# Two down projections by seven block products instead of eight

## The reference

```python
def swiglu(x, w_gu, w_down):
    g, u = jnp.split(x @ w_gu, 2, axis=-1)
    return (jax.nn.silu(g) * u) @ w_down

# second_block
f = swiglu(rms_norm_2(h, ffn1_pre_g[i]), ffn1_w_gu[i], ffn1_w_down[i])
h = h + 0.5 * rms_norm_2(f, ffn1_post_g[i])
z = rms_norm_2(h, attn_pre_g[i]) @ w_in[i] + b_in[i]
...
f = swiglu(rms_norm_2(h, ffn2_pre_g[i]), ffn2_w_gu[i], ffn2_w_down[i])
h = h + 0.5 * rms_norm_2(f, ffn2_post_g[i])
gate = jax.nn.sigmoid(rms_norm_2(h, ple_pre_g[i]) @ w_ple_gate[i])
```

## Time and profile before

| | us |
|---|---|
| median of 3 runs (lowest, highest) | 3358.51 (3353.12, 3361.56) |
| profiled execution, its own time | 3359.73 |
| its span, first to last instruction | 3357.9 |
| PE busy | 3182.2 (95%) |
| DVE, ACT, POOL busy | 1837.1, 1250.6, 1771.7 |

### The profile page before, as it was taken

How to read it: one execution, slowest core, us unless ns; L and a number is a source line. 1 busy time by engine, 2 the same in 40 slices (tenths; PEclk the granted TensorE clock), 3 DMA queues, 4 the chain that set the end, 5 groups by cost and what they waited for, 6 DMA issues and landing times.

```text
span 3357.9 us, 41185 instructions
## 1 busy us (share of the span) xinstructions
PE 3182.2 (95%) x15279; PEld 2617.1 (78%) x15279; DVE 1837.1 (55%) x2613; ACT 1250.6 (37%) x2354; POOL 1771.7 (53%) x1314
## 2 busy tenths in 40 slices
PE   6978889899999999999999999989998999999998
PEld 4865578678887887888888888878877888888876
DVE  6779772799997133755541331167737655533124
ACT  4136372555453122433331231167714433322132
POOL 3331046655556777554467652344366554567653
PEclk8979899999999999999999999999999999999999
DMA  5534524323333533222335424546442323245333
GB/s 198 123 103 139 133 64 169 138 82 94 108 93 119 197 140 100 77 81 86 121 119 200 150 88 142 188 111 154 101 179 66 95 80 128 76 165 211 112 112 120
DMA packets 309011, 416.72 MB, mean 124 GB/s; under 512 B 59767, under 2 KB 231994, under 8 KB 306532
## 3 DMA queue, kind: packets, MB, share of 16 engines
q1 hardware_dynamic: 239768, 242.51, 24.3%
q10 hardware_dynamic: 64108, 154.67, 12.4%
q0 software_dynamic: 4960, 17.22, 1.6%
HBM read 326.88 MB, written 93.75 MB: 125 GB/s over the span
## 4 chain that ended last, share of the span: by engine, by line
PE 80%; DVE 9%; issue 4%; ACT 3%; POOL 2%; DMA 1%; ACTq 0%; SPq 0%; DVEq 0%; POOLq 0%
PE PS L911 71%; PE PS L2385 3%; PE PS L2402 1%; PE PS L2369 1%; PE PS L848 1%; DVE pt L781 1%; ACT act L803 1%; POOL dg_ab L2560 1%; DMA w_raw<-w_out 0%; PE PS L437 0%; DVE h_lo L905 0%; PE PS L460 0%; DVE px L784 0%; ACT gs__259 L1926 0%; DVE pr_ab L2502 0%
## 5 line engine op out<-in xcount | busy, mean ns | idle before, releaser
L1258 POOL TENSOR_TENSOR sl<-ss,sh 128x512 fp32r<-128x512 f32 x300 | 454.5, 1527 | 533.7 <-ACT sh L1249 533.7
L290 POOL TENSOR_TENSOR w_lo<-w_raw,w_hi 128x512 fp32r<-128x512 f32 x460 | 658.2, 1462 | 16.0
L286 POOL CAST w_hi<-w_raw 128x2048 fp32r<-128x2048 f32 x115 | 226.5, 1970 | 588.0 <-DMA w_raw<-w_in 195.4
L1480 DVE TENSOR_TENSOR cset<-cset,PS 128x512 f32<-128x512 f32 x360 | 235.9, 683 | 345.2 <-PE PS L911 345.1
L911 PE MATMUL PS<-h_hi,sh 128*128 128x512 f32 x960 | 374.8, 390 | 3.0 <-issue 2.5
L911 PE MATMUL PS<-h_lo,sh 128*128 128x512 f32 x960 | 374.1, 390 | 0.0
L911 PE MATMUL PS<-h_hi,sl 128*128 128x512 f32 x960 | 374.0, 390 | 0.0
L985 DVE TENSOR_TENSOR a_lo<-aT,a_hi 128x1024 fp32r<-128x1024 f32 x66 | 108.9, 1653 | 458.3 <-ACT a_hi L982 458.3
L1237 DVE TENSOR_TENSOR ss<-sr 128x512 f32<-128x512 f32 x300 | 331.0, 1104 | 0.3 <-issue 0.3
L911 PE MATMUL PS<-w_hi,a_hi 128*128 128x512 f32 x1056 | 326.3, 390 | 5.0 <-DVE a_lo L985 5.0
L911 PE MATMUL PS<-w_hi,a_lo 128*128 128x512 f32 x1056 | 325.6, 389 | 0.0
(11 more groups left out here) (356 smaller groups left out, 6496.5 us busy)
## 6 DMA issues: line engine op xcount, KB each, us to landing
w_raw<-ffn_w_down SPq DMA_DIRECT2D x88, 512.0 KB, 4.3
sr<-ffn_w_gu SPq DMA_DIRECT2D x80, 512.0 KB, 5.1
ad<-cset ACTq DMA_DIRECT2D x66, 512.0 KB, 3.1
w_raw<-w_down SPq DMA_DIRECT2D x44, 512.0 KB, 4.3
xs<-px ACTq DMA_DIRECT2D x40, 512.0 KB, 3.3
sr<-w_up SPq DMA_DIRECT2D x40, 512.0 KB, 5.1
w_raw<-w_out SPq DMA_DIRECT2D x32, 512.0 KB, 4.7
w_raw<-w_in SPq DMA_DIRECT2D x28, 512.0 KB, 5.3
```

Of the source, the lines that this page charges most:

```text
L286: e.tensor_copy(w_hi[b][:, 0:n], w_raw[b][:, 0:n]).then_inc(S("w_hi"), 1)
L290: op = e.tensor_tensor(w_lo[b][:, s], w_raw[b][:, s], w_hi[b][:, s].bitcast(F32), ALU.subtract)
L1258: e.tensor_tensor(s.lo[p][:], src, s.hi[p][:].bitcast(F32), ALU.subtract).then_inc(S("s_op"), 1)
L1480: e.tensor_tensor(out, out, PS[:, b, :], op).then_inc(S("s_ev"), 1)
```

## The change

Down projections p = 2 and p = 4 (f = 1, 2) are cut into blocks: rows of the result 0 to 511 and 512 to 1023, columns 0 to 511 and 512 to 1023, and of the inner dimension the even and the odd 128-tiles (11 each). The four result blocks come from seven products of block sums (q = 0 to 6; `W_OF` lists the weight's side) instead of eight products.

- A product is 11 steps of 12 matmuls (4 row tiles, three matmuls each); a down projection has `NS` = 77 steps, numbered s.
- The activation's sums are made in the up projection: DVE adds five 128x512 operations for each two i (`pair_even_dve`, `pair_odd_dve`), ACT stores all seven variants in DRAM (`sd`); in `copies_act` two of the PSUM copies change places and wait for these sums too. SP loads one 128x512 tile per step back (6 slots), ACT and DVE split it.
- The weight is loaded once and stays in SBUF (`w_rows`). Per step DVE makes the weight's sum (in five of the seven products), ACT its hi, POOL its lo part (4 slots).
- Results leave PSUM after each product: ACT copies them to `yacc` in SBUF or DVE adds them there (24 operations of DVE and 16 of ACT for each down projection).
- The post of rows 0 to 3 moves to steps 62 to 68 of DVE and 60 to 71 of ACT.
- Of the next stage's weight only one chunk is loaded and split ahead; the others are loaded after the last step.

```diff
+        W_OF = (("11", "22", ALU.add), ("21", "11", ALU.subtract), ("21", "22", ALU.add), ("12", "22", ALU.subtract),
+                ("22",), ("11", "12", ALU.add), ("11",))
...
+        def a_slot_free(e, f, s):
+            if s < 6:
+                up_done(e, f, (0, 1, 2, 5, 6, 7)[s])
+            else:
+                step_done(e, f, s - 6)
+        def w_slot_free(e, f, s):
+            if s < 4:
+                up_done(e, f, (3, 4, 7, 7)[s])
+            else:
+                step_done(e, f, s - 4)
...
+        def seven_load_a(e, f, s):
+            q, j = s // KP, s % KP
+            a_slot_free(e, f, s)
+            if q == 0:
+                e.wait_ge(S("a_st1"), stores(f, j + 1))
+            elif j == 0:
+                stores_landed(e, f)
+            if s > 4:
+                a_landed(e, f, s - 5)
+            e.dma_start(sevens[f].a_raw[s % 6][:], sd[:, q, j, :]).then_inc(S(TILE[s % 5]), 16)
+        def seven_sp(e, f):
+            for s in range(NS):
+                if s < KP:
+                    seven_load_w(e, f, s)
+                seven_load_a(e, f, s)
+                if s == KP - 1:
+                    for i in range(KP, KP + 3):
+                        seven_load_w(e, f, i)
+                elif s == KP + 3:
+                    for i in range(KP + 3, KP + 5):
+                        seven_load_w(e, f, i)
+                elif s == 4 * KP:
+                    stream_load(e, G_UP[f] + CL, G_UP[f] + CL + 1)
...
+        def seven_pool(e, f):
+            for s in range(NS):
+                seven_w_low(e, f, s)
+                if s == NS - 10:
+                    stream_split(e, G_UP[f] + CL, G_UP[f] + CL + 1)
...
+        def seven_dve(e, f):
+            p = P_OF[f]
+            for s in range(6, NS):
+                q = s // KP - 1
+                if s % KP == 4 and q in (2, 4, 5):
+                    for i in range(4):
+                        seven_sum_dve(e, f, q, i)
+                if s in (62, 64, 66, 68):
+                    post_dve(e, p, (s - 62) // 2)
...
+                seven_step_dve(e, f, s)
+            tail_dve(e, p)
...
         def tail_dve(e, p):
+            if p in SEVEN:
+                f = 1 + SEVEN[p]
+                seven_sum_dve(e, f, 6, 0)
+                seven_sum_dve(e, f, 6, 1)
+                post_dve(e, p, 4)
+                seven_sum_dve(e, f, 6, 2)
+                post_dve(e, p, 5)
+                seven_sum_dve(e, f, 6, 3)
...
             norm_out_dve(e, p + 1, 0)
...
-                    e.wait_ge(S("n_tmp"), 37 + i)
+                    e.wait_ge(S("d_ev"), 48)
```

More of the change, by code:

```diff
@@ L1425, in up_act @@
                     ahead(p)
-                if i == 14:
+                if i == 14 and not f:
                     a_back_act(e, f, 0)
+                if i == FT - 1 and f:
+                    for s_ in range(2):
+                        seven_a_high(e, f, s_)
+                    for s_ in range(2):
+                        seven_w_high(e, f, s_)
                 e.wait_ge(S("s_ev"), 6 * n + 3)
@@ L1459, in up_dve @@
                 weight_sum_dve(e, f, 0, 5)
+                pair_even_dve(e, f, 0)
+                for k in range(4):
+                    pair_odd_dve(e, f, 0, k)
                 weight_sum_dve(e, f, 0, 6)
@@ L1492, in up_dve @@
                 ahead(3)
+                if i == FT - 1 and f:
+                    for s_ in range(2):
+                        seven_w_sum(e, f, s_)
+                        seven_a_low(e, f, s_)
                 e.wait_ge(S("s_pd"), 7 * n + 5)
@@ L1509, in up_dve @@
                 ahead(6)
+                if i == FT - 1 and f:
+                    seven_step_dve(e, f, 2)
                 if f:
@@ L1513, in up_dve @@
                     e.tensor_tensor(gate, gate, val, ALU.mult).then_inc(S("f_out"), 1)
+                    if i % 2 == 0:
+                        pair_even_dve(e, f, i // 2)
+                    else:
+                        for k in range(4):
+                            if i == FT - 1 and k < 3:
+                                seven_step_dve(e, f, 3 + k)
+                            pair_odd_dve(e, f, i // 2, k)
                 else:
@@ new lines, in pair_odd_dve @@
+        def pair_odd_dve(e, f, j, k):
+            a, b = cset[0][:, 0], cset[1][:, 0]
+            e.wait_ge(S("f_out"), 3 + FT * f + 2 * j + 1)
+            e.wait_ge(S("a_st1"), stores(f, j))
+            to, x, y, op = ((0, a[:, 0], b[:, 1], ALU.add), (2, a[:, 0], b[:, 0], ALU.add), (3, a[:, 1], b[:, 1], ALU.add),
+                            (1, b[:, 0], b[:, 1], ALU.subtract))[k]
+            e.tensor_tensor(st_odd[:, to], x, y, op).then_inc(S("d_sm"), 1)
+        KP = FT // 2
+        NS = 7 * KP
@@ new lines, in build, with seven_copy_act, seven_sum_dve, add @@
+        y_part = lambda T, c: yacc[:, T, c * 512:(c + 1) * 512]
+        def seven_copy_act(e, f, q):
+            F = f - 1
+            for i in range(4):
+                e.wait_ge(S("d_pd"), 98 * F + 14 * q + 10 + i + 1)
+                src = PS[:, BLOCK[BLOCK_OF[q]][i], :]
+                for T, c in {0: ((i, 0), (4 + i, 1)), 1: ((4 + i, 0),), 3: ((i, 1),)}[q]:
+                    e.activation(y_part(T, c), src, ACT.Copy).then_inc(S("d_ac"), 1)
+        def seven_sum_dve(e, f, q, i):
+            F = f - 1
+            e.wait_ge(S("d_pd"), 98 * F + 14 * q + 10 + i + 1)
+            src = PS[:, BLOCK[BLOCK_OF[q]][i], :]
+            def add(T, c, op):
+                e.tensor_tensor(y_part(T, c), y_part(T, c), src, op).then_inc(S("d_ev"), 1)
+            if q == 2:
+                e.wait_ge(S("d_ac"), 16 * F + 2 * i + 2)
+                add(i, 0, ALU.add)
+            elif q == 4:
+                e.wait_ge(S("d_ac"), 16 * F + 12 + i + 1)
+                add(i, 1, ALU.add)
+                e.wait_ge(S("d_ev"), 24 * F + i + 1)
+                add(i, 0, ALU.subtract)
+            elif q == 5:
+                e.wait_ge(S("d_ac"), 16 * F + 2 * i + 2)
+                add(4 + i, 1, ALU.add)
+            else:
+                e.wait_ge(S("d_ac"), 16 * F + 8 + i + 1)
+                add(4 + i, 0, ALU.add)
+                e.wait_ge(S("d_ev"), 24 * F + 12 + i + 1)
+                add(4 + i, 1, ALU.subtract)
```

305 lines of the change are left out of this document (249 added, 56 removed).

## The result

| | before | after |
|---|---|---|
| median of 6 runs each (lowest, highest), us | 3358.26 (3353.12, 3361.56) | 3372.03 (3367.64, 3379.07) |
| span of the profiled execution, us | 3357.9 | 3370.8 |

What follows compares the result with a forecast made beforehand. PE was taken to bound the kernel, busy for 95% of the span. -59.8 + 17.2 + 14.0 + 3.4 = -25.2 from 3359.7 gives 3334.5, stated as 3333 us; range 3308 to 3370, the forecast's own 3322 to 3345.

Steps and rivals of the forecast that it cites:

- PE's saving: Both changed down projections: 132 fewer matmuls each at 0.2265 us, 29.9 us each, 59.8 us saved in all.
- The step's balance: Down projection steps with a weight's sum: DVE and POOL together need 2.5 to 2.66 us against PE's 2.72; 0 lost.
- rival 2: Down projections: DVE and POOL bound the steps, 3.2 us instead of 2.72, 53 us lost, about 3385; chance 0.14.
- The up projection: DVE's added sums hide behind its wait for PE: cost 0, or 40 us if cover failed by 1 us per i.
- Rival 4: Up projection waits for stores or sums, 0.5 us in each of 40 i: 3353; at 1 us, 3373; chance 0.07.
- Loads near step 11: Down projection: step 11's tile, last of 3.25 MB in one queue, comes late; 1.1 us each time (0 to 6).
- q = 5: Down projection, steps 59 to 68: DVE's eight additions, then posts, exceed its reserve; 4.7 us each time (0 to 12).
- POOL's split: Product 6, between steps 67 and 68: splitting the next stage's chunk outlasts the reserve; 1.5 us each (0 to 5).
- Start of the down projection: Step 6 is ready 17.6 us after the start and wanted at 16.3: 1.3 us each time (0 to 3).
- The hand-over: Down projection to next stage: PE waits for `h_lo` behind DVE's additions and posts; 8.0 and 6.0, together 14.0 us (10 to 18).
- The clock: PE's lower clock behind each hand-over's wait of 8 us: 1.7 us each, 3.4 in all (0 to 7).
- rival 3: Bursts twice as dear (34 us), hand-over at its upper bound, clock half for longer: -2 to -15, about 3350; chance 0.12.

Runs made afterwards that it cites:

- The edit of ACT's order: Changed kernel, with ACT making two hi parts ahead of its wait for the first store at the second and third up projections' start: 3369.9 us, 1.0021.
- the kernel with small additions: Changed kernel, but DVE's eight additions of product 6 do 8 of 512 columns, so the result lacks most of that product: 3366.57 us, 1.0022.
- the two moves of DVE's posts: Each against the changed kernel: rows 4 to 7 behind the next stage's lo parts, 3376.61 us; rows 0 to 3 at steps 66 to 69, 3372.09 us.
- the second try: Changed kernel, with late weight loads at steps 10, 12, 14, 22 and 27 and the residual's load at step 40, not 20: 3361.12 us, 1.0000.
- the one with four edits: Changed kernel with ACT's hi parts earlier, loads spread, POOL's split behind the last step, posts at steps 66 to 69: 3340.26 us, then 3343.99.

## Why the prediction was wrong

- **PE's saving, 59.8 us: right.** The matmul's pitch stayed at 0.2265 us, and 264 are gone.
- **The step's balance, cost 0: right.** 40 steps without a pause; rival 2 is refuted. Times of DVE and POOL add up, as read from the 2588 us stretch, and POOL's median `dwl` is 1.29 to 1.30 us, as reckoned.
- **The up projection, cost 0: wrong, +6.1 and +6.5 us.** The step was "Behind them wait ACT's store and the last two copies from PSUM; PE wants those banks back only a whole i later". That is true of every i but the first: there ACT's queue also holds the hi parts for PE's next products. The middle of the up projection costs nothing. Of the 6.1 and 6.5 us, 2.8 and 4.3 are more idle time of PE, and the rest is busy time at the lower clock. The edit of ACT's order took 1.6 us off each pause; what makes the rest of them late was not settled. Rival 4 had the right stage, but its 0.5 us in each i is not what happened.
- **Loads near step 11, 1.1 us each: mis-sized, 5.38 and 4.20.** The stores' landing was right to 0.1 us. The forecast had everything issued at once; SP took 4.36 us to issue six loads, the tile's own issue came 4.5 us behind the first of them, and it landed 13.1 us behind it instead of 10.4. Whether the issuing or other traffic made the difference was not tried. In the six kernels that share these loads the pause is 3.4 to 5.4 us in down p = 2 and 3.6 to 4.9 in down p = 4, so the 5.38 is at the upper end of what this place costs. The bound of 6 held. The spread loads gave back 12 us.
- **q = 5, 4.7 us: the sum is right, 4.5 both times, its parts in part by luck.** Forecast were 2.4 us ahead of steps 62 and 64 and catching up from 66 on; the pauses stand ahead of 62, 64 and 66 with 1.5, 1.7 and 1.3, and the post ahead of 66 took 4.5 us instead of 3.4.
- **POOL's split, 1.5 us each: mis-sized, 5.6, beyond its bound of 5.** The price 6.9 us was taken from a place without a post beside it, although the sum itself had a post there and the adding up was known. Moving it gave back 14 us, more than the 9 us of pause.
- **Start of the down projection, 1.3 us: 0.3.**
- **The hand-over, 8.0 and 6.0: 9.0 and 6.5**, by the pauses (9.83 for 0.84; 9.78 and 1.56 for 0.84, 0.34, 1.56 and 2.10), 15.5 together and within 10 to 18. (The prediction's terms add up to 9.3 us after the end, not 9.4.) That the additions make half of it is shown by the kernel with small additions; that the posts make the other half is read from DVE's timeline, and no run takes them out.
- **The clock, 3.4 us, only behind the hand-over: wrong.** Behind the hand-overs the lower level outlasts the pause by 3.2 and 4.7 us, an estimated 4 us lost in all, so that price was near. But the down projections lose 4.2 + 4.2 = 8.4 us to it, and the up projections 2.4 and 2.3 us behind their first i, where the sum has nothing. With the split and the first i this is the step that failed: the earlier trace rows showed that a pause of 6.3 us brings 1.2 GHz behind it, and that price was set to one kind of pause only, while the terms 1.1 and 1.5 were too small to raise the question.

In all: the down projections' pauses are 30.8 us instead of 17.2 (+13.6), their clock 8.4 instead of 0, and 3.6 are the short delays at both ends of the 13 pauses and what rounding leaves, which makes the 25.6 that the table shows; the up projections are +12.6; the stretch behind down p = 2 is 3.6 and the rest 0.5 above the forecast; 4.2 us came off ahead of the change. That is the distance from -25.2 to +12.9. In the stretch behind down p = 2 the lower clock is also longer in code that is unchanged; what of the 3.6 us the change causes stays open. In kind it was rival 3, "bursts twice as dear": its 34 us for the bursts are near the 30.8 measured. Its far end, 2 us under the kernel before, is passed by 15 us, most of which are the up projections.

## What to carry to other kernels

Follow every engine in order through the first and last turn of a loop, not only through its middle: a wait that the steady state hides stands in full where the engine's next work is wanted at once. When a kernel runs PE at 100%, a pause of 4 us or more cost its own length and then 1.5 to 2.8 us of work at 1.2 GHz behind it, and many of 2 to 4 us did so too, so price each pause with that. Work moved to a time at which its engine or queue is free pays (POOL's split, the loads); work moved within a stretch in which its engine is the bound moves the pause (the two moves of DVE's posts).

## What the runs showed of the hardware that was not expected

- A load of 2 MB on ACT's queue and 1.5 MB of weight on SP's, 2 us apart, made ACT wait 6.20 us for a tile of 256 KB that otherwise lands in 2.7 us (median). Moved apart (the second try) the same loads made it wait at most 1.07 us behind the weight and 2.65 us behind the 2 MB, which its reserve hides: PE's pauses there are 0.5 us and less.
- Two kernels that are the same up to a place can differ there: the wait for `x_lo` in the first i of f = 1 is 2.6 us in five of the kernels and at most 1.1 in the others, with the next wait shorter or longer in exchange. Each kernel has one trace, apart from the one with four edits, whose two agree (1.08 us), so whether the kernel or the single execution makes this stays open.
